# Two decoder layers on one core: the first value projections taken from the un-normalized stream

## The chip, the cores and the metric

One Trainium2 chip, one of its cores. The metric is device microseconds of one execution of the whole kernel. Three runs of the kernel before gave a median of 1659.62 us (1659.4 to 1661.38).

## The reference, cut to what matters

Two layers over 512 tokens of width 1024, each a pre-norm mixer with a plain residual add, and a final norm. Everything is float32.

```python
def rmsnorm(x, g):
    y = x * lax.rsqrt(jnp.mean(x * x, axis=-1, keepdims=True) + EPS)
    return y * g

for i in range(2):
    u = rmsnorm(h, ln_g[i])
    # layer 0, HGRN2:     q, f_pre, i_in (the values), gate = columns of u @ hg_w_in
    #                     chunkwise gated recurrence per head, norm per head, * silu(gate), @ hg_w_out
    # layer 1, attention: for 3 groups (window, dilation): q, k, v = columns of u @ att_w_in
    #                     16 heads of 128; dilated attention, merged over groups, * silu(gate), @ att_w_out
    h = h + y
return rmsnorm(h, final_g)
```

## The kernel before

The stream is held transposed, `hT` with 8 tiles of 128 features by 512 tokens. A float32 product is made of three fp32r matmuls (`split_matmuls`, L428): each operand is split in a high part (ScalarE, a copy that rounds: `split_hi` L741, `u_high` L757) and a low part (VectorE, the difference: `split_lo` L1030, in `norm` L1044). TensorE multiplies high by high, high by low and low by high. The kernel is written engine by engine, each with its instructions in a fixed order, tied by semaphores; no scheduler moves anything.

Weights come in tiles of 128 by 1024 (512 KB), four slots deep, from SyncE's queue: a slot is loaded again when its low part exists (`load_after` L336), and split again when TensorE has used the tile (`wait_tile_done` L285).

The 16 heads go in four groups of four (`quads` L268). Both layers begin with a prologue in which the values of the first four heads are projected: `first_values` (L470) goes over k, the 8 feature tiles, outside and over s, the four results, inside: 3 matmuls for each (k, s), 12 per k, 96 in all. Layer 1 (AT) has three value groups: group 0 by `first_values`, groups 1 and 2 by `values` (L449), which takes s outside and k inside. Groups 1 and 2 take every fourth token. ScalarE copies each result out of PSUM (`copy_values` L750), which counts up `bank_free` of the event's bank. Projections take three banks (`proj`) in turn, by the event's number. A head tile (`head_tile` L436, 24 matmuls) waits for its weight tile and for its bank:

```python
pe.wait_ge(w_ready, number + 1)
pe.wait_ge(bank_free[bank], before)
```

**Opening.** x comes in four tiles of 128 tokens (`load_x` L355), is transposed by TensorE (L554), copied to `hT` by VectorE (L1075), squared and summed by ScalarE (L777); the factor rstd of every token is spread over the partitions by one matmul (L561). Then `norm(0)` makes u = hT * gain * rstd, tile by tile (L1051, L759, L1056), and `first_values` follows it. Midway `bias_rows` (L491) makes the rows of the attention bias; VectorE adds a mask to them (L1109).

**Between the layers.** The last quad's output projection is done in two stages: heads 0 to 2, then head 3 alone, 8 columns of 3 matmuls (`out_projection` L529). VectorE adds each column to `hT` (`add_out` L1217), ScalarE squares it (`square_column` L761), TensorE sums the squares over the features (`sum_squares` L538, one float32 matmul with a matrix of ones). After the eighth sum ScalarE makes rstd (L894, L896), `norm(1)` makes u, and layer 1's `first_values` begins.

## Time and profile before

| | |
|---|---|
| median of three runs | 1659.62 us (1659.4 to 1661.38) |
| the profiled execution | 1660.9 us |
| its span, first to last instruction | 1658.9 us |
| granted TensorE clock, mean | 0.996 |
| TensorE busy | 1634.7 us (99%), 8249 matmuls |
| VectorE busy | 800.4 us (48%) |
| ScalarE busy | 641.3 us (39%) |

A matmul's record is longer than the time it takes from the stream (about 0.39 us against 0.23 from start to start), since records overlap; so times of TensorE are read below from start to start. An instruction with float32 operands has two records. "Granted clock" is the share of full speed, 1.0 for 2.4 GHz and 0.5 for 1.2 GHz.

### The profile page before, as it was taken

What the parts mean: (1) busy time and instruction counts of PE and PEld (TensorE: products, weight loads), DVE (VectorE), ACT (ScalarE), POOL (GpSimd) and SP (SyncE); (2) the same over time, 40 slices, a digit from 0 to 9 for tenths busy, and PEclk for the clock granted to TensorE, in tenths of its full rate; (3) what the DMA queues carried; (4) which work ended last, traced back from release to release, by engine and by line L of the source; (5) the groups of instructions that cost most, each with busy time, mean ns of one, the idle gap of its engine ahead of it and who ended that gap; (6) DMA issues with size and microseconds to landing.
All of it is one profiled execution on the core that took longest, in us unless ns stands there. A gap on an engine that the chain in (4) does not pass through costs nothing.

```text
span 1658.9 us, 22066 instructions
## 1 busy us (share of the span) xinstructions
PE 1634.7 (99%) x8249; PEld 1392.4 (84%) x8249; DVE 800.4 (48%) x1395; ACT 641.3 (39%) x1088; POOL 20.8 (1%) x40
## 2 busy tenths in 40 slices
PE   7999999999999999999999999999999999999997
PEld 5888888888886898888898888899888889888886
DVE  6674675575576424444323444333344432443445
ACT  4553453453454333333332343332343332233333
POOL 0000000000000000000000000000000000000000
PEclk9999999999999999999999999999999999999999
DMA  6523223323221344333333333323323332343311
GB/s 202 177 77 100 78 76 89 89 76 89 82 80 42 89 113 96 79 84 61 104 96 96 96 83 89 78 70 118 91 64 92 96 70 89 114 96 85 82 52 64
DMA packets 247997, 149.46 MB, mean 90 GB/s; under 512 B 47040, under 2 KB 227648, under 8 KB 247920
## 3 DMA queue, kind: packets, MB, share of 16 engines
q1 hardware_dynamic: 203328, 139.69, 30.5%
q0 software_dynamic: 2608, 8.39, 1.5%
q10 hardware_dynamic: 41984, 0.27, 1.3%
q8 instruction: 59, 0.97, 0.2%
q14 instruction: 18, 0.15, 0.0%
HBM read 146.02 MB, written 6.50 MB: 92 GB/s over the span
## 4 chain that ended last, share of the span: by engine, by line
PE 96%; DVE 2%; ACT 1%; issue 0%; DMA 0%; SPq 0%; DVEq 0%; ACTq 0%
PE proj L432 82%; PE inner L699 3%; PE inner L667 2%; PE inner L432 2%; PE inner L687 2%; PE inner L655 1%; PE inner L576 1%; PE inner L599 1%; PE inner L602 1%; PE inner L588 1%; PE inner L581 0%; DMA v<-x 0%; DVE v L1421 0%; PE inner L554 0%; PE inner L541 0%
## 5 line engine op out<-in xcount | busy, mean ns | idle before, releaser
L1036 DVE TENSOR_TENSOR w_lo<-raw,w_hi 128x1024 fp32r<-128x1024 f32 x252 | 308.0, 1223 | 484.0 <-ACT w_hi L748 483.0
L432 PE MATMUL proj<-u_hi,w_hi 128*128 128x512 f32 x1280 | 509.7, 398 | 0.0
L432 PE MATMUL proj<-u_hi,w_lo 128*128 128x512 f32 x1280 | 500.2, 391 | 0.0
L432 PE MATMUL proj<-u_lo,w_hi 128*128 128x512 f32 x1280 | 498.9, 390 | 0.0
L748 ACT ACTIVATE w_hi<-raw 128x1024 fp32r<-128x1024 f32 x252 | 265.3, 1053 | 133.6 <-PE proj L432 118.5
L432 PEld LDWEIGHTS proj<-u_hi,w_lo 128*128 128x128 f32 x1280 | 240.3, 188 | 51.7
L432 PEld LDWEIGHTS proj<-u_lo,w_hi 128*128 128x128 f32 x1280 | 240.9, 188 | 48.0
L432 PEld LDWEIGHTS proj<-u_hi,w_hi 128*128 128x128 f32 x1280 | 240.7, 188 | 47.4
L432 PE MATMUL proj<-w_hi,u_hi 128*128 128x512 f32 x472 | 190.2, 403 | 6.7 <-issue 3.7
L432 PE MATMUL proj<-w_lo,u_hi 128*128 128x512 f32 x472 | 187.5, 397 | 0.0
L432 PE MATMUL proj<-w_hi,u_lo 128*128 128x512 f32 x472 | 187.4, 397 | 0.0
L432 PEld LDWEIGHTS proj<-w_hi,u_hi 128*128 128x128 f32 x472 | 120.8, 256 | 19.7 <-issue 8.9
L432 PEld LDWEIGHTS proj<-w_hi,u_lo 128*128 128x128 f32 x472 | 120.8, 256 | 9.1
L432 PEld LDWEIGHTS proj<-w_lo,u_hi 128*128 128x128 f32 x472 | 121.0, 256 | 8.0
L982 ACT ACTIVATE qk<-proj 128x512 f32<-128x512 f32 x96 | 57.0, 594 | 162.6 <-PE proj L432 162.0
L912 ACT ACTIVATE rows<-rows,negm 128x256 f32<-128x256 f32 (+1 forms) x128 | 61.8, 484 | 140.9 <-DVE negm L1319 130.6
L432 PE MATMUL proj<-y_hi,w_hi 128*128 128x512 f32 x256 | 102.9, 402 | 0.9 <-DVE sg L1125 0.7
L432 PE MATMUL proj<-y_hi,w_lo 128*128 128x512 f32 x256 | 99.8, 390 | 0.0
L432 PE MATMUL proj<-y_lo,w_hi 128*128 128x512 f32 x256 | 99.8, 390 | 0.0
L754 ACT ACTIVATE v<-proj 128x512 f32<-128x512 f32 x59 | 35.1, 596 | 138.8 <-PE proj L432 127.2
L1221 DVE TENSOR_TENSOR hT<-hT,proj 128x512 f32<-128x512 f32 x80 | 54.4, 686 | 65.6 <-PE proj L432 65.4
L432 PEld LDWEIGHTS proj<-y_hi,w_hi 128*128 128x128 f32 x256 | 48.1, 188 | 12.3 <-issue 3.0
(162 smaller groups left out, 1420.9 us busy)
## 6 DMA issues: line engine op xcount, KB each, us to landing
raw<-at_w_in SPq DMA_DIRECT2D x160, 512.0 KB, 4.1
raw<-hg_w_in SPq DMA_DIRECT2D x64, 512.0 KB, 4.2
raw<-hg_w_out SPq DMA_DIRECT2D x16, 512.0 KB, 3.5
raw<-at_w_out SPq DMA_DIRECT2D x16, 512.0 KB, 4.4
v<-x SPq DMA_DIRECT2D x4, 512.0 KB, 6.4
bias_tiles<-ext_rows POOLq DMA_DIRECT2D x1, 2048.0 KB, 11.8
bias_tiles<-ext_rows POOLq DMA_DIRECT2D x2, 1024.0 KB, 17.2
bias_n<-bias_tiles POOLq DMA_DIRECT2D x16, 128.0 KB, 4.0
```

The costliest lines, as they stand in the source:

```text
L432: ins = nc.tensor.matmul(bank[:, :], stationary(a), moving(b), start=(first and n == 0), stop=(last and n == 2))
L576: ins = nc.tensor.matmul(to, aft[:, b * P + c * CH:b * P + (c + 1) * CH], q_steps(b, 0, c, NC - c), start=True, stop=True)
L588: ins = nc.tensor.matmul(p_U[:, b * P:(b + 1) * P], kT[:, b, :], v_sb[0][:, b, h * P:(h + 1) * P], start=True, stop=True)
L667: ins = nc.tensor.matmul(p_S[r // 2][:, ((r % 2) * 2 + i) * P:((r % 2) * 2 + i + 1) * P], qk[:, 2 + 2 * i, s], qk[:, 3 + 2 * i, s], start= ...
L687: ins = nc.tensor.transpose(p_T[n % 2][:, (i % 4) * P:(i % 4 + 1) * P], src, ident[:, :])
L699: ins = nc.tensor.matmul(o, vals, pT[:, i, :], start=(i == 0), stop=(i == len(TILES) - 1), skip_group_check=True)
L748: nc.scalar.activation(w["hi"][:, slot, :], raw[:, slot, :], ACT.Copy).then_inc(hi_ready, 1)
L754: nc.scalar.activation(v_sb[group][:, (e - (0 if q is None else layer.heads)) % ST, :], value_bank(layer, q, e)[:, :], ACT.Copy).then_inc( ...
L912: nc.scalar.activation(probs[:, i, 0:n], probs[:, i, 0:n], ACT.Exp, bias=negm[:, i:i + 1], accum_out=stat[:, i // ST, 1, b:b + 1]).then_in ...
L982: nc.scalar.activation(o, src, ACT.Copy, scale=QSCALE if i in (Q0, Q1, Q2) else 1.0)\
L1036: nc.vector.tensor_tensor(w["lo"][:, slot, :], raw[:, slot, :], w["hi"][:, slot, :].bitcast(F32), ALU.subtract).then_inc(w_ready, 1)
L1221: nc.vector.tensor_tensor(hT[:, k, :], hT[:, k, :], proj[bank][:, :], ALU.add)\
```

## The change

The norm multiplies each token by rstd and each feature by a gain. For a value projection the token is the output's row, so rstd can be applied to the result. The change splits hT * gain, without rstd, for the values of layer 0 and for groups 0 and 1 of layer 1, and gives rstd as a per-partition scale to the copy out of PSUM. The normalized u is made afterwards, for the heads (and group 2), over the same buffers, each pair of tiles when TensorE has used it. In detail:

- x goes in half tiles: 4 transposes, ScalarE copies them to `hT`, VectorE multiplies by the gain, ScalarE and VectorE split. TensorE's transposes and value steps alternate. The gains come by a small load of their own, and the first weight tile is loaded ahead of x's tiles 1 to 3.
- ScalarE's squares of x, rstd and its spreading follow after x's splits. `bias_rows` stands before k = 7.
- Between the layers, squares are added up on VectorE (7 adds). Eight float32 matmuls with one moving column give the sum for every token as a column (`token_sum`), and one of 512 columns the sum spread over the partitions (`feature_sum`).
- Value steps of layer 1 begin between columns 5 and 6 of the output projection's second stage. Group 1 is taken with k outside, too. Group 0 gets banks `inner[0..3]`, the last of group 1 `inner[4]`.

```diff
@@ loads, SyncE @@
             load_x(0)
             sp.dma_start(ident[:, :], consts[:, 0:P]).then_inc(const_loaded[0], 16)
+            sp.dma_start(prow[0:16, P:2 * P], ln_g.rearrange("r (h p) -> (r h) p", p=P)).then_inc(const_loaded[3], 16)
+            load(0, *tile_source(HG, 0, "value", 0, 0))
             for t in range(1, ST):
                 load_x(t)
+            for n in range(1, SLOTS):
+                load(n, *tile_source(HG, 0, "value", 0, n))
...
-            for n in range(SLOTS):
-                load(n, *tile_source(HG, 0, "value", 0, n))
@@ TensorE @@
-            def first_values(layer, u_before):
...
+            def value_step(layer, group, k, s):
+                number, slot, _ = layer.tile(None, 4 * group + k // 2)
+                e = 4 * group + s
+                _, bank, before = layer.event(None, e)
+                if k % 2 == 0 and s == 0:
+                    pe.wait_ge(w_ready, number + 1)
+                if layer is HG and k % 4 == 0:
+                    pe.wait_ge(raw_ready, k + s + 1)
+                elif layer is AT and group == 0 and s == 0:
+                    pe.wait_ge(raw_ready, KT + k + 1)
+                if k == 0 and layer is AT and value_bank(layer, None, e) is proj[bank]:
+                    pe.wait_ge(bank_free[bank], before)
...
+            def token_sum():
+                pe.wait_ge(sq_added, KT - 1)
+                for i in range(2 * ST):
+                    tokens = slice(i * P, (i + 1) * P) if i < ST else slice(i - ST, S, RES)
+                    ins = nc.tensor.matmul(p_ss[:, i:i + 1], sq_sum[:, tokens], ones[:, 0:1], start=True, stop=True)
+            def feature_sum():
+                pe.wait_ge(rcol_step, 1)
+                nc.tensor.matmul(p_ss[:, :], ones[:, :], sq_sum[:, :], start=True, stop=True).then_inc(feature_sums, 1)
...
+                    if last and layer is HG and c == 5:
+                        value_step(AT, 0, 0, 0)
+                        value_step(AT, 0, 0, 1)
...
+            pe.wait_ge(diag_ready, 1)
+            nc.tensor.matmul(p_ss[:, :], ones[:, :], y_f[:, :], start=True, stop=True).then_inc(rstd_spread, 1)
+            bias_rows()
+            for s in range(ST):
+                value_step(HG, 0, 7, s)
@@ ScalarE @@
             def u_high(which, k):
+                wait_tile_done(act, AT if which else HG, None, 4 * which + k // 2, False)
                 act.wait_ge(u_made, which * KT + k + 1)
...
+            def first_value_events(layer, group):
+                last_raw = layer is HG or group == 1
                 for i in range(3):
+                    if last_raw:
+                        u_high(group, 2 * i)
+                        u_high(group, 2 * i + 1)
+                    split_hi(layer, None, 4 * group + i, False)
                 for s in range(ST):
+                    copy_values(layer, None, group, 4 * group + s)
+                if last_raw:
+                    u_high(group, KT - 2)
+                    u_high(group, KT - 1)
+                split_hi(layer, None, 4 * group + 3, False)
...
+            act.wait_ge(feature_sums, 1)
             nc.scalar.activation(rstd[:, :], p_ss[:, :], ACT.Ln, scale=1.0 / D, bias=eps[:, :]).then_inc(rstd_step, 1)
...
+            first_value_events(AT, 0)
+            first_value_events(AT, 1)
+            value_events(AT, None, 2, 0)
@@ VectorE @@
-            norm(0)
...
                 nc.vector.tensor_tensor(ext_sb[:, g * EXT:(g + 1) * EXT], inner[1 + g][0:H, 0:EXT],
                                         relmask_sb[:, g * EXT:(g + 1) * EXT], ALU.add).then_inc(ext_ready, 1)
-            for n in range(3):
-                split_lo(HG, None, n, False)
+            norm(0)
...
+            def last_shares(q):
+                column(0); column(1); raw_low(0); column(2); split_lo(HG, q, HG.heads, True)
+                column(3); column(4); column(5); column(6); raw_low(1); column(7); raw_low(2)
...
+                split_lo(HG, q, HG.heads + 3, True)
+                raw_low(7)
+                add_squares(5)
+                add_squares(6)
+                add_squares(7)
```

(`last_shares` has one call per line in the kernel; its calls are drawn together here.)

Three places of the new order, in which instructions stand otherwise than before.

VectorE, from the end of the parameter arithmetic in the opening. L1109 and L1263 are the mask adds on the rows of `bias_rows`, L1159 and L1164 the two halves of `norm`, L1036 and L1144 `split_lo`. Before:

```order
L1104 TENSOR_SCALAR oml<-lb 128x16 [waits lb_step]
L1109 TENSOR_TENSOR qx<-inner,qx 16x384 [waits ext_done,const_loaded6,lb_step]
L1109 TENSOR_TENSOR qx<-inner,qx 16x384 [waits ext_done] x2
L1036 TENSOR_TENSOR w_lo<-raw,w_hi 128x1024 [waits hi_ready] x3
L1113 MEMSET rows 128x512
```

And with the change:

```order
L1258 TENSOR_SCALAR oml<-lb 128x16 [waits lb_step]
L1263 TENSOR_TENSOR qx<-inner,qx 16x384 [waits ext_done,const_loaded6,lb_step]
L1263 TENSOR_TENSOR qx<-inner,qx 16x384 [waits ext_done] x2
L1159 SCALAR_TENSOR_TENSOR tmp<-hT,param,rstd 128x512 [waits rstd_ready]
L1159 SCALAR_TENSOR_TENSOR tmp<-hT,param,rstd 128x512
L1164 TENSOR_TENSOR u_lo<-tmp,u_hi 128x512 [waits u_hi_ready]
L1159 SCALAR_TENSOR_TENSOR tmp<-hT,param,rstd 128x512 [waits u_ready]
L1164 TENSOR_TENSOR u_lo<-tmp,u_hi 128x512 [waits u_hi_ready]
L1144 TENSOR_TENSOR w_lo<-raw,w_hi 128x1024 [waits hi_ready]
```

The whole of `norm(0)` now stands behind the mask adds, which wait for `bias_rows`; before it stood ahead of the parameter arithmetic.

ScalarE, the copies of the first values in the opening (L754, L817) and what stands ahead of them (L759, L824 are `u_high`; L748, L809 `split_hi`). Before:

```order
L759 ACTIVATE u_hi<-tmp 128x512 [waits u_made] x2
L791 ACTIVATE param<-param 128x48 [waits lb_step]
L811 ACTIVATE ones_r<-ones 128x128 [waits ones_ready]
L748 ACTIVATE w_hi<-raw 128x1024 [waits value_tile_done,loaded0]
L748 ACTIVATE w_hi<-raw 128x1024 [waits value_tile_done,loaded1]
L748 ACTIVATE w_hi<-raw 128x1024 [waits value_tile_done,loaded2]
L754 ACTIVATE v<-proj 128x512 [waits proj_done] x3
```

And with the change:

```order
L889 ACTIVATE rstd<-inner 128x512 [waits rstd_spread]
L916 ACTIVATE ones_r<-ones 128x128 [waits ones_ready]
L824 ACTIVATE u_hi<-tmp 128x512 [waits u_made,value_tile_done] x2
L809 ACTIVATE w_hi<-raw 128x1024 [waits value_tile_done,loaded0]
L824 ACTIVATE u_hi<-tmp 128x512 [waits u_made,value_tile_done] x2
L809 ACTIVATE w_hi<-raw 128x1024 [waits value_tile_done,loaded1]
L824 ACTIVATE u_hi<-tmp 128x512 [waits u_made,value_tile_done] x2
L809 ACTIVATE w_hi<-raw 128x1024 [waits value_tile_done,loaded2]
L817 ACTIVATE v<-proj,cols 128x512 [waits proj_done] x3
```

Six of the eight `u_high` now stand ahead of the copies out of PSUM.

ScalarE, from rstd to layer 1's first value copies. Before:

```order
L894 ACTIVATE rstd<-inner,eps 128x512 [waits ss_done]
L896 ACTIVATE rstd<-rstd 128x512 [waits rstd_step]
L759 ACTIVATE u_hi<-tmp 128x512 [waits u_made] x2
L748 ACTIVATE w_hi<-raw 128x1024 [waits proj_done,loaded2]
L759 ACTIVATE u_hi<-tmp 128x512 [waits u_made] x2
```

And with the change:

```order
L1001 ACTIVATE cols<-inner,eps 128x8 [waits token_sums]
L1004 ACTIVATE cols<-cols 128x8 [waits rcol_step]
L1006 ACTIVATE rstd<-inner,eps 128x512 [waits feature_sums]
L1008 ACTIVATE rstd<-rstd 128x512 [waits rstd_step]
L809 ACTIVATE w_hi<-raw 128x1024 [waits value_tile_done,loaded0,rcol_ready]
L809 ACTIVATE w_hi<-raw 128x1024 [waits value_tile_done,loaded1]
L809 ACTIVATE w_hi<-raw 128x1024 [waits value_tile_done,loaded2]
L817 ACTIVATE v<-inner,cols 128x512 [waits proj_done] x4
```

The splits of group 1's weights and the copies of group 0's values now stand behind a wait for `feature_sum`, which TensorE does just before k = 7.

## Rows read from the trace of the kernel before

**Rows 1.** The page: busy time and share of the span of each engine.
```profile
PE 1634.7 (99%) x8249; PEld 1392.4 (84%) x8249; DVE 800.4 (48%) x1395; ACT 641.3 (39%) x1088; POOL 20.8 (1%) x40
```
**Rows 2.** Waits of TensorE, whole span: us in total, times, longest.
```profile
PE proj L432 <- issue: 3.7, 1, 3.7
PE proj L432 <- DVE u_lo L1056: 3.0, 1, 3.0
```
**Rows 3.** Timeline, 0 to 20 us: start, us, engine, line, operation.
```profile
7.82 5.26 PE L554 MATMUL inner<-ident,v 128*128 128x128 f32 x24 [1.43 <-DMA v<-x]
...
10.45 1.06 ACT L777 ACTIVATE rows<-v 128x1024 f32<-128x1024 f32 x1 [0.19 <-DMA v<-x]
...
15.60 1.41 DVE L1051 SCALAR_TENSOR_TENSOR tmp<-hT,param,rstd 128x512 f32<-128x512 f32 x2
...
17.89 0.77 PE L432 MATMUL proj<-w_hi,u_hi 128*128 128x512 f32 x1 [3.04 <-DVE u_lo L1056]
```
**Rows 4.** Timeline, 22 to 45 us.
```profile
23.12 0.40 PE L432 MATMUL proj<-w_hi,u_hi 128*128 128x512 f32 x1
...
25.29 1.04 ACT L770 ACTIVATE w_hi<-raw 128x1024 fp32r<-128x1024 f32 x1
...
31.41 2.10 PE L496 MATMUL inner<-rows,bias_n 32*16 32x384 f32 x6
...
33.45 0.51 PE L432 MATMUL proj<-w_hi,u_hi 128*128 128x512 f32 x1
...
34.03 2.34 DVE L1036 TENSOR_TENSOR w_lo<-raw,w_hi 128x1024 fp32r<-128x1024 f32 x2
```
**Rows 5.** Timeline of TensorE, first matmuls of head tiles 0 and 1.
```profile
44.50 0.39 PE L432 MATMUL proj<-u_hi,w_hi 128*128 128x512 f32 x1
...
49.94 0.39 PE L432 MATMUL proj<-u_hi,w_hi 128*128 128x512 f32 x1
```
**Rows 6.** Windows: length, busy time and count of each engine, granted clock.
```profile
18.00:20.00 2.00, 2.00 (x5) 1.61 (x6) 2.00 (x3) 1.19 (x2) 0.00 (x0) 0.50 0.63 168
```
**Rows 7.** Timeline between the layers, 526 to 566 us.
```profile
526.76 1.13 PE L541 MATMUL inner<-tmp,ones 128*128 128x512 f32 x2
...
528.42 1.02 PE L541 MATMUL inner<-tmp,ones 128*128 128x512 f32 x2
...
529.51 0.39 PE L432 MATMUL proj<-y_lo,w_hi 128*128 128x512 f32 x1
...
538.31 0.69 ACT L894 ACTIVATE rstd<-inner,eps 128x512 f32<-128x512 f32 x1 [0.27 <-PE inner L541]
539.03 0.63 ACT L896 ACTIVATE rstd<-rstd 128x512 f32<-128x512 f32 x1
...
541.93 0.77 PE L432 MATMUL proj<-w_hi,u_hi 128*128 128x512 f32 x1 [3.66 <-issue]
...
545.64 0.39 PE L432 MATMUL inner<-w_hi,u_hi 128*128 128x512 f32 x1
...
565.37 0.40 PE L432 MATMUL proj<-w_hi,u_hi 128*128 128x512 f32 x1
...
565.57 0.60 ACT L754 ACTIVATE v<-inner 128x512 f32<-128x512 f32 x1
```
**Rows 8.** Groups of instructions, 505 to 542 us: busy, mean ns, idle before.
```profile
L1221 DVE TENSOR_TENSOR hT<-hT,proj 128x512 f32<-128x512 f32 x16 | 10.7, 682 | 4.7 <-PE proj L432 4.6
...
L766 ACT ACTIVATE tmp<-hT 128x512 f32<-128x512 f32 x8 | 5.0, 631 | 11.1 <-DVE hT L1221 7.9 <-PE inner L541 3.1
L1036 DVE TENSOR_TENSOR w_lo<-raw,w_hi 128x1024 fp32r<-128x1024 f32 x4 | 4.9, 1221 | 3.7 <-ACT w_hi L748 3.7
...
L1051 DVE SCALAR_TENSOR_TENSOR tmp<-hT,param,rstd 128x512 f32<-128x512 f32 x3 | 2.2, 751 | 0.4 <-ACT rstd L896 0.4
```
**Rows 9.** Timeline: six records of three small float32 matmuls, and what follows.
```profile
508.48 0.94 PE L588 MATMUL inner<-v,kT 128*128 128x128 f32 x6 [0.52 <-ACT kT L817]
...
509.17 0.48 PE L432 MATMUL proj<-y_hi,w_hi 128*128 128x512 f32 x1
```

More of the change, by code:

```diff
@@ L434, in split_matmuls, with head_tile @@
                 return ins
[L436 removed]
+            def head_tile(layer, q, n, half, first=False):
                 number, slot, _ = layer.tile(q, n)
@@ L533, in out_projection @@
                     out_column(layer, q, tile + c // 2, tile + c + (KT if last else 0), c, (HQ - 1,) if last else range(HQ))
[L534 to L542 removed]
+                    if last and layer is AT and c >= 2:
+                        final_transposes(c - 2)
@@ L556, in _ @@
-            for i in (1, 2, 3):
-                pe.wait_ge(const_loaded[i], 16)
-            nc.tensor.transpose(proj[0][:, 0:80], prow[0:80, 0:P], ident[0:80, 0:80]).then_inc(param_T, 1)
+                if n >= 3:
+                    pe.wait_ge(x_copied, n - 2)
+                for i in range(4):
+                    ins = nc.tensor.transpose(inner[1 + n % 3][:, i * P:(i + 1) * P],
+                                              nat[t][:, half, i * P:(i + 1) * P], ident[:, :])
+                ins.then_inc(x_T, 1)
@@ new lines, in _ @@
+            x_transposes(1, 1)
+            value_step(HG, 0, 0, 3)
+            value_step(HG, 0, 1, 3)
+            x_transposes(1, 2)
+            for s in range(ST):
+                value_step(HG, 0, 2, s)
+                if s == 0:
+                    x_transposes(1, 3)
+            for s in range(ST):
+                value_step(HG, 0, 3, s)
+            for i in (1, 2):
+                pe.wait_ge(const_loaded[i], 16)
+            nc.tensor.transpose(p_ss[:, 0:64], prow[0:64, 0:P], ident[0:64, 0:64]).then_inc(param_T, 1)
@@ L625, in hg_body @@
                     for half in range(2 * HG.per_head):
-                        head_tile(HG, q, HG.per_head * h + half // 2, half % 2)
+                        head_tile(HG, q, HG.per_head * h + half // 2, half % 2, first=(h == 0 and half < 2))
                         if h:
@@ L1290, in hg_body @@
                         split_lo(HG, q, HG.heads + n, last)
-                out_shares(HG, q, last)
+                if last:
+                    last_shares(q)
+                else:
+                    out_shares(HG, q, last)
                 assert links == LINKS_HG, links
             quads(dve, hg_body)
+            for n in range(4):
+                split_lo(AT, None, n, False)
             norm(1)
-            for n in range(AT.pro):
+            for n in range(8, AT.pro):
                 split_lo(AT, None, n, False)
```

287 lines of the change are left out of this document (195 added, 92 removed).

## The prediction

> **What bounds the kernel now.** I read the page first: TensorE is busy for 1634.7 us [rows 1] of a span of 1658.9, and no other engine for half of it. So only what TensorE does not do, or does slowly, can be won. Its waits name two places: 3.0 us in the opening, for the first low part of u, and 3.7 us between the layers [rows 2]. The timeline shows what lies around each. In the opening the first value matmul starts at 17.89 [rows 3], though the last tile of x had landed by 10.4 (ScalarE squares it at 10.45 [rows 3]); between stand rstd, its spreading and the first tile of u. Between the layers the eighth sum of squares, rstd (0.69 + 0.63) and u come one after the other until 541.93 [rows 7]. The windows show the granted clock at 0.50 (1.2 GHz) after the first wait [rows 6], and the starts give the price: 12 matmuls from 17.89 to 23.12 took 5.23 us [rows 3, 4], where 24 take 5.44 in head tile 0, 0.227 each [rows 5], so 2.5 us went there; 9 matmuls from 541.93 to 545.64 took 3.71 instead of 2.04 [rows 7], so 1.7 there. A sum of squares costs TensorE 0.86: from 528.42 to 529.51 less one matmul of 0.23 [rows 7].
>
> **The sum.** I follow TensorE in both places and compare the start of a later instruction: the end of head tile 0 in the opening (49.94 before [rows 5]), and the start of value group 1 between the layers (565.37 before [rows 7]). Behind both the matmuls are the same and no wait of weight is known.
>
> *Opening, up to the bias rows.* The first weight tile now stands ahead of x's tiles 1 to 3, so tile 2 lands when tile 3 did, by 10.4. Three groups of transposes are queued ahead of the first value matmul, which can start at 11.2. Call B the time at which `bias_rows` starts. Until then TensorE does 84 of the 96 matmuls (19.1), 20 transposes (24 took 5.26 [rows 3], at the pace of VectorE's copies, so 0.22 each, 4.4, is the upper end, and half of it the lower; I take 3.0), the parameter transpose (0.2) and rstd's spreading (0.9, as a sum of squares). The clock has fallen by then or falls: 1.7 to 2.5 us as priced, 2.0 taken. Small waits: 0.5. B = 11.2 + 19.1 + 3.0 + 0.2 + 0.9 + 2.0 + 0.5 = 36.9. ScalarE gives nearly the same: from x's arrival on it has 8 copies (0.60), 8 high parts (0.63), 4 squares (1.06, with the read of the sum some 1.25) and 4 weight splits (1.04), so the fourth weight tile's low part is there at about 33.4, and k = 6, the bias and spreading follow. Bounds of B: 34.5 (no low clock, quick transposes) to 39.5 (low clock until the last of x).
>
> *From B to head tile 0.* TensorE does the bias rows (2.04, 31.41 to 33.45 [rows 4]) and k = 7 (2.73) and is free at B + 4.8. But head tile 0 waits for its bank, which is the one of the second value result, and ScalarE copies that only behind six `u_high` and three splits. These follow `norm(0)`, which VectorE starts behind the mask adds. The rows price each link: from the start of the bias rows to VectorE's next work behind the mask adds 2.6 (31.41 to 34.03 [rows 4]); from the first multiply of `norm` to the end of ScalarE's third split behind six high parts 10.7 (15.60 [rows 3] to 25.29 + 1.04 [rows 4]), the same alternation as now; then two copies of 0.60 [rows 7] and 0.06 for the scale read from memory. So head tile 0 starts at B + 14.6, after a wait of 9.8 us. That wait is longer than both waits after which the clock fell, so 2.0 more (1.7 to 2.5) on 5.44. The last two tiles of u are in time, since the head tile needs them 4 us after its start. End of head tile 0: 36.9 + 14.6 + 5.4 + 2.0 = 58.9, against 49.94: **9.0 us lost** (bounds 6.3 to 12.1, by B and the clock).
>
> On the scale, ScalarE's Ln with a bias from memory takes 0.69 and Exp without one 0.63 [rows 7]. The Trainium skill (ScalarE: Activation LUTs, What ACT_TABLE_LOAD costs) gives 93 ns for each such operand. By the row the two copies ahead of head tile 0 take 0.12 longer, by the page 0.19; the measured row is used.
>
> *Between the layers.* Before, from the end of column 2 at 526.52 (the last matmul ahead of 526.76 [rows 7]) to 565.37, 38.85 us held 15 + 96 matmuls, 25.2, and 13.6 of other things: eight sums of squares 6.9, the wait of 3.7, the low clock 1.7, small gaps 1.3. All 13.6 go. What comes:
> - Column 5 waits for VectorE to add column 2, and the first value step for its weight's low part, both behind a split of 1.22 and a `raw_low` of 0.75 [rows 8]: 0.8.
> - `token_sum` waits for the seventh add. VectorE has 8 column adds (0.68), 8 `raw_low` (0.75), 4 splits (1.22) and 7 adds (0.68), 21 us by their records [rows 8], some 19 from start to start as records overlap; and with two buffers for squares an add, a square, a high part and a low part follow each other in a ring between two engines, three times, 1.4 each. From 525.4 that ends at 548.4; TensorE gets there at 547.1: 1.4 (0 to 3).
> - `token_sum` itself: 16 records; 6 such took 0.69 (508.48 to 509.17 [rows 9]): 1.8. `feature_sum`: 0.9.
> - Group 1 waits for ScalarE. Behind `feature_sum` it does Ln and Exp (1.3 [rows 7]), three splits (3.0) and two copies (1.3), and only then is group 1's first bank free, for the count of that bank takes in group 0's second copy: 5.8 with the hops. TensorE has only k = 7 to do, 2.7. Wait: 3.1.
> - Group 2's last weight tile comes 0.2 late, being split behind the last two high parts.
>
> In all 8.2, so **5.4 us gained** (bounds 3.5 to 7.5). The adds and low parts that VectorE gains, and `norm(1)`, lie beside 22 us of group 1; if that cover were gone `norm` would cost its 14 us.
>
> *Sum:* +9.0 - 5.4 = +3.6 us. The profiled execution took 1660.9 (span 1658.9 and 2.0 around it); it would take 1664.5. The median of the runs is 1.3 below it, 1659.6, so I predict **1663.2 us**. A measurement of this kernel can tell a change of 0.2%, 3.3 us, from none.
>
> **The rivals.**
>
> *A second fall of the clock.* The wait ahead of group 1, 3.1 us, is as long as the 3.0 after which 12 matmuls ran at 1.2 GHz [rows 2, 3]. If the clock falls there too it costs 1.7 more: 1664.9; if instead the low clock lasts through x's arrival (B = 39.5, 2.6 later) 1665.8. For it: both waits of this length in the trace ended so. Against: TensorE is dense up to this one. The Trainium skill (TensorE: Matmul & The Clock Gate, Loop structure matters more than you think) says that matmuls between waits run at half clock; the two rows agree with it.
>
> *A quick opening.* B at 34.5 and the short low-clock price give +6.5 there, +1.1 in all: 1660.7. For it: the transposes' 0.22 was the copies' pace, not their own. Against: ScalarE's own sum allows B no earlier than about 36, unless its records overlap more than in the opening before.
>
> *No wait ahead of head tile 0* (the other side). If the copy that frees the bank, and u, do not come behind `norm(0)`'s chain, TensorE goes from k = 7 at B + 4.8 straight on: 9.8 and the clock's 2.0 are not lost, and the change is 8.2 faster, 1651.4. For it: everything else in the change is saving. The point: 3.6 + 3.3 = 6.9 of the 11.8 (wait and clock) have to go, so it decides where the wait, with what the clock costs behind it, is under 4.9 us. Against: the order of instructions on VectorE and ScalarE, which no run can alter, and the 10.7 us of rows 3 and 4.
>
> *The change does less than it says between the layers*: a ring of waits on VectorE holds value steps up too, each k then taking VectorE's 2.8 instead of 2.73 and more; up to 3 us worse, 1666.
>
> **How the numbers follow.** The forecast, +3.6 with its own range 1661.0 to 1665.5, has a chance of 0.45. The second fall or a long low clock 0.20; the quick opening 0.20; no wait ahead of head tile 0 0.08; the slow ring 0.07. The limit of "slower" at 1662.9 cuts the forecast: 0.6 of it lies above. Slower: 0.27 + 0.20 + 0.07 = 0.54, less a little for errors common to all: 0.52. Within 0.2%: 0.18 + 0.20 = 0.38. Faster: 0.08, and 0.02 for what I have not seen: 0.10. The range, 1659.3 to 1668.0, leaves out the fast case and the bounds added one on the other.
>
> **What would show each step.** In the changed profile: the first value matmul at about 11; the bias rows at 36 to 38; TensorE idle for 10 us ahead of head tile 0's first matmul (L442) near 51, released by ScalarE's value copy (L817); VectorE's first `norm` multiply 2.6 us behind the bias rows. Between the layers no idle time ahead of the first value step beyond 1 us, one of about 1.4 ahead of L510 and one of about 3 ahead of group 1, released by ScalarE's L817; the start of group 1 less the end of head tile 0 should be 5.2 smaller than the 515.4 before (the last 0.2 lies behind it). The prediction is wrong if the wait ahead of head tile 0 is under 5 us, or if the time between those two marks shrinks by more than 8 us.

## The result, and the profile after

| | before | after |
|---|---|---|
| time, median of the runs | 1661.01 us (1659.4 to 1661.38, 6 runs) | 1667.79 us (1666.62 to 1669.89, 6 runs) |
| ratio to before, 95% interval | | 1.0044 (1.0034 to 1.0055) |
| profiled execution | 1660.9, span 1658.9 | 1669.1, span 1667.2 |

The change costs 6.8 us by the medians and 8.2 by the two profiled executions; 3.6 was predicted. Ratios are of fast runs only; the one slow run of all is one of `sums_spread`, at 1818.3 us, without which its median is 1663.97. The page after, the busy row: VectorE has 24 operations more [rows 1], TensorE is as busy as before.

```profile
PE 1634.6 (98%) x8252; PEld 1392.3 (84%) x8252; DVE 815.3 (49%) x1419; ACT 653.9 (39%) x1114; POOL 20.9 (1%) x40
```

TensorE's waits after, whole span (us in total, times, longest), answer to [rows 2]. Both waits of before are gone, and one of 9.6 us has come, with two smaller ones.

```profile
PE proj L442 <- ACT v L817: 12.4, 2, 9.6
...
PE inner L510 <- DVE rows L1182: 1.2, 1, 1.2
```

*The opening.* Timelines after, of TensorE, VectorE and ScalarE, against [rows 3 to 5]:

```profile
11.09 0.78 PE L442 MATMUL proj<-w_hi,u_hi 128*128 128x512 f32 x1
...
36.18 2.10 PE L524 MATMUL inner<-rows,bias_n 32*16 32x384 f32 x6
...
38.80 1.39 DVE L1159 SCALAR_TENSOR_TENSOR tmp<-hT,param,rstd 128x512 f32<-128x512 f32 x2
...
49.53 1.83 ACT L817 ACTIVATE v<-proj,cols 128x512 f32<-128x512 f32 x3
...
50.83 0.80 PE L442 MATMUL proj<-u_hi,w_hi 128*128 128x512 f32 x1 [9.59 <-ACT v L817]
...
55.61 0.39 PE L442 MATMUL proj<-u_hi,w_lo 128*128 128x512 f32 x1
```

The first value matmul comes 6.8 us sooner than before, and then the chain runs as it was priced: bias rows at 36.18, the norm 2.62 behind them, ScalarE's value copies at 49.53, head tile 0 at 50.83 after a wait of 9.59. Up to 55 us its matmuls stand 0.43 apart instead of 0.227. The first recurrence starts at 72.27, where before it started at 63.63: **8.6 us lost**. Its row after, and before:

```profile
72.27 1.06 PE L630 MATMUL inner<-qx,aft 128*32 128x128 f32 x32
```

```profile
63.63 1.06 PE L576 MATMUL inner<-qx,aft 128*32 128x128 f32 x32
```

*Between the layers*, against [rows 7]. Timelines after, of TensorE and ScalarE:

```profile
557.27 2.92 PE L510 MATMUL inner<-ones,rows 128*128 128x1 f32 x16 [1.19 <-DVE rows L1182]
560.05 0.47 PE L442 MATMUL inner<-w_hi,u_hi 128*128 128x512 f32 x1
...
561.37 0.63 PE L442 MATMUL inner<-w_lo,u_hi 128*128 128x512 f32 x1
...
564.47 1.02 PE L516 MATMUL inner<-rows,ones 128*128 128x512 f32 x2
...
566.78 2.93 ACT L809 ACTIVATE w_hi<-raw 128x1024 fp32r<-128x1024 f32 x3
...
569.62 2.40 ACT L817 ACTIVATE v<-inner,cols 128x512 f32<-128x512 f32 x4
...
571.01 0.79 PE L442 MATMUL proj<-w_hi,u_hi 128*128 128x512 f32 x1 [2.79 <-ACT v L817]
```

And windows after, of TensorE: the stretch, its length, busy time, matmuls, granted clock, share and rate of the DMA engines.

```profile
557.00:560.00 3.00, 2.73 (x16) 1.00 0.16 59
560.00:561.00 1.00, 1.00 (x5) 0.83 0.00 0
561.00:564.00 3.00, 3.00 (x9) 0.50 0.00 0
...
572.00:574.00 2.00, 2.00 (x6) 0.50 0.90 316
```

The clock falls twice. It is full during the one-column matmuls and at 0.50 (1.2 GHz) soon behind them; then again behind the wait for group 1. Each time the matmuls at 0.43 cost 1.6 to 1.7 us. Layer 1's heads start at 617.90, against 610.48: of the 8.6 us, 7.4 are still there. **Between the layers 1.2 us came back, not 5.4.** The first matmul of the heads after, and before:

```profile
617.90 0.39 PE L442 MATMUL proj<-u_hi,w_hi 128*128 128x512 f32 x1
```

```profile
610.48 0.40 PE L432 MATMUL proj<-u_hi,w_hi 128*128 128x512 f32 x1
```

### The profile page after: what moved, and what is told of

The parts are those of the page before. It is cut to its first block, busy times and chain, and to the rows that moved or that the text cites. A ratio compares the mean times of both kernels' runs of the same rounds, so it can differ in the third digit from the quotient of the medians.

```text
span 1667.2 us, 22147 instructions
## 1 busy us (share of the span) xinstructions
PE 1634.6 (98%) x8252; PEld 1392.3 (84%) x8252; DVE 815.3 (49%) x1419; ACT 653.9 (39%) x1114; POOL 20.9 (1%) x40
## 4 chain that ended last, share of the span: by engine, by line
PE 95%; DVE 3%; ACT 1%; issue 1%; DMA 0%; SPq 0%; DVEq 0%; ACTq 0%
PE proj L442 80%; PE inner L760 3%; PE inner L442 2%; PE inner L728 2%; PE inner L748 2%; PE inner L716 1%; PE inner L630 1%; PE inner L653 1%; PE inner L656 1%; PE inner L642 1%; PE inner L635 0%; DMA v<-x 0%; DVE w_lo L1144 0%; DVE v L1607 0%; DVE rows L1182 0%
## 5 line engine op out<-in xcount | busy, mean ns | idle before, releaser
L1144 DVE TENSOR_TENSOR w_lo<-raw,w_hi 128x1024 fp32r<-128x1024 f32 x252 | 308.0, 1223 | 457.4 <-ACT w_hi L809 456.6
L809 ACT ACTIVATE w_hi<-raw 128x1024 fp32r<-128x1024 f32 x252 | 265.1, 1053 | 120.6 <-PE proj L442 117.1
L442 PE MATMUL proj<-w_hi,u_hi 128*128 128x512 f32 x440 | 178.4, 406 | 3.0 <-ACT v L817 2.8
L442 PE MATMUL proj<-w_lo,u_hi 128*128 128x512 f32 x440 | 175.0, 398 | 0.0
L442 PE MATMUL proj<-w_hi,u_lo 128*128 128x512 f32 x440 | 175.0, 398 | 0.0
L442 PEld LDWEIGHTS proj<-w_hi,u_hi 128*128 128x128 f32 x440 | 114.2, 260 | 14.1 <-DVE w_lo L1144 5.3
L442 PEld LDWEIGHTS proj<-w_hi,u_lo 128*128 128x128 f32 x440 | 114.2, 260 | 8.1
L442 PEld LDWEIGHTS proj<-w_lo,u_hi 128*128 128x128 f32 x440 | 114.5, 260 | 7.0
L817 ACT ACTIVATE v<-proj 128x512 f32<-128x512 f32 x49 | 29.2, 596 | 119.1 <-PE proj L442 107.9
```

The costliest lines, as they stand in the source:

```text
L442: ins = nc.tensor.matmul(bank[:, :], stationary(a), moving(b), start=(first and n == 0), stop=(last and n == 2))
L809: nc.scalar.activation(w["hi"][:, slot, :], raw[:, slot, :], ACT.Copy).then_inc(hi_ready, 1)
L817: nc.scalar.activation(v_sb[group][:, s, :], value_bank(layer, q, e)[:, :], ACT.Copy, scale=cols[:, 8 + ST * group + s:9 + ST * group + s] ...
L1144: nc.vector.tensor_tensor(w["lo"][:, slot, :], raw[:, slot, :], w["hi"][:, slot, :].bitcast(F32), ALU.subtract).then_inc(w_ready, 1)
```

## The experiments

Two kernels first undo one half of the change each; then single parts are moved, and at last two are put together. Each ratio is to the kernel before, in runs on the same chip. A difference to the change in us, where no span is named, compares medians of different chips, on which the kernel before took 1660.68 to 1661.47; such a difference of less than 1 us is not read.

### 1 and 2. One half of the change at a time

`opening_undone` has the whole opening of the kernel before, x's loads, transposes and norm included (a few lines of many):

```
-                raw_u = q is None and group < 2
+                raw_u = layer is AT and q is None and group < 2
...
-            bias_rows()
-            for s in range(ST):
-                value_step(HG, 0, 7, s)
+            pe.wait_ge(param_ready, 1)
+            first_values(HG, 0)
```

> The opening as before, the place between the layers as changed. If the two places simply add up (mine): the changed kernel's profile has head tile 0 end 8.6 us later than before, and the start of layer 1's heads 7.4 us later, so the opening costs 8.6 and the place between the layers gives back 1.3. Then this kernel's head tile 0 ends at 49.9, layer 1's heads begin at about 609.2, and the time is 1.3 us or less under the kernel before, no measurable change. Rival: the two falls of the clock between the layers come from where the opening has shifted that place in time; then without the shift one or both are missing and the kernel is 3 to 4.5 us faster than before.

Measured: 1659.51 us (11 runs; before 1661.47), ratio 0.9990 (0.9981 to 0.9999). The rival is out: both low stretches between the layers are there without the shift, as these windows show, behind the same waits of 1.2 and 2.8 us.

```profile
551.00:554.00 3.00, 3.00 (x10) 0.59 0.00 0
562.00:564.00 2.00, 2.00 (x6) 0.50 1.02 373
```

The heads of layer 1 start at 608.63, 1.9 us sooner than before. Of that, 0.7 was there already at the first recurrence (62.91 against 63.63), ahead of which the two kernels have the same code; 1.1 to 1.2 came between the layers, as in the change.

`between_undone` has the new opening, and between the layers the code of the kernel before:

```
-                raw_u = q is None and group < 2
+                raw_u = layer is HG and q is None and group < 2
...
-                    if last and layer is HG and c == 5:
-
-                        value_step(AT, 0, 0, 0)
-                        value_step(AT, 0, 0, 1)
+                        (sum_squares if layer is HG else final_transposes)(c - 2)
```

> The opening as changed, the place between the layers as before. If the two places add up: 8.6 to 8.7 us slower than the kernel before (about 1669.7), slower than the whole change; head tile 0 starts at 50.8 behind a wait of 9.6. Rival: ScalarE and VectorE run late by the opening's shift only there, and steady work in the loops takes part of it back; then under 6 us.

Measured: 1669.68 us (5 runs), ratio 1.0047 (1.0034 to 1.0061), 7.8 to 8.2 more than before. Its first wait is 9.59 us, as in the change, and the rival of under 6 us is out. So the opening alone loses 8, the part between the layers alone gains 1 to 2, and the two add up to the 6.8 of the change within the noise. Of the two halves the opening went as predicted; the mistake is between the layers.

### 3. Value copies early

The four copies of the first values right behind the first two `u_high` and one split.

```
-                for s in range(ST):
-                    copy_values(layer, None, group, 4 * group + s)
+                    if layer is HG and i == 0:
+                        for s in range(ST):
+                            copy_values(layer, None, group, s)
...
```

> The changed kernel, but ScalarE copies the four first value results behind the first two high parts of u instead of behind six. If the bank is what head tile 0 waits for: it starts near 43.5 instead of 50.8, is then held by u tile by tile (the low parts come every 1.9 us), and ends near 55 instead of 58.6: 3.6 us less, or 2 if the thin stream of matmuls keeps the clock low into head tile 1. Rival: u, not the bank, ends that wait as well; then the start stays near 50 and the time does not change.

Measured: 1667.27 us (1664.89 to 1668.38), ratio 1.0032 (1.0019 to 1.0046), which overlaps with the change's; its span is 1.8 less than the change's. The timelines of this kernel:

```profile
43.31 0.47 PE L442 MATMUL proj<-u_hi,w_hi 128*128 128x512 f32 x1 [2.51 <-DVE w_lo L1148]
...
52.61 0.50 PE L442 MATMUL proj<-u_hi,w_hi 128*128 128x512 f32 x1 [1.44 <-DVE u_lo L1168]
...
61.01 1.06 ACT L809 ACTIVATE w_hi<-raw 128x1024 fp32r<-128x1024 f32 x1 [3.35 <-DMA raw<-hg_w_in]
...
68.98 1.06 PE L630 MATMUL inner<-qx,aft 128*32 128x128 f32 x32 [0.91 <-DVE qx L1346]
```

Head tile 0 starts 7.5 us sooner and ends 4.3 sooner (54.27 against 58.58): it now waits for the norm inside itself, column by column. Then ScalarE waits 3.35 us for a weight tile that it had waited 0.85 for in the change, and the first recurrence is 3.3 sooner. Of that 1.5 are lost between the layers, 0.85 of it behind the one-column matmuls: there the clock fell at once, and the stretch from them to `feature_sum` took 5.27 us (556.93 to 562.20) instead of 4.42. So the first theory had the start and the end of head tile 0 (43.5 and 55 expected), and the norm as the next limit. It did not have the weights behind it, nor that the clock's price between the layers can change with nothing moved there.

### 4. Weight splits ahead of the sums

Between the layers, ScalarE's three splits for group 1 ahead of its wait for `feature_sum`.

```
+            for i in range(3):
+                split_hi(AT, None, i, False)
             act.wait_ge(feature_sums, 1)
...
-                    split_hi(layer, None, 4 * group + i, False)
+                    if last_raw:
+                        split_hi(layer, None, 4 * group + i, False)
```

> The changed kernel, but between the layers ScalarE splits group 1's first three weight tiles ahead of the wait for feature_sum instead of behind it. If the wait ahead of group 1 is ScalarE's queue: its copies of group 0 are then done by about the end of k = 7, the wait of 2.8 us shrinks under 0.5, and the fall of the clock behind it (1.6 us) goes with it: 4 us less. Rival: the clock falls there for another reason (the falls follow the load, not the wait); then only 2.5 us less.

Measured: 1664.29 us (10 runs), ratio 1.0016 (1.0007 to 1.0025), 3.5 less than the change and 4.6 by the span. Group 1 starts without a wait, and the windows show the clock full there, but still low behind `token_sum`:

```profile
567.67 0.60 PE L442 MATMUL proj<-w_hi,u_hi 128*128 128x512 f32 x1
```

```profile
561.00:564.00 3.00, 3.00 (x10) 0.58 0.22 20
...
568.00:570.00 2.00, 2.00 (x10) 1.00 0.35 132
```

The second fall belonged to the wait; with the wait it is gone, as the first theory says.

### 5. Two of the eight token sums

This kernel leaves out the sums of six of the eight columns, so it sizes a cost and is no version to use.

```
-                for i in range(2 * ST):
+                for i in (0, ST):
```

> The changed kernel, but token_sum issues only two of its eight matmuls with one moving column (the first of the plain and the first of the strided four), so the row factors of six of the eight value row blocks are not computed: that part is left out. It sizes two things that the sum had wrong or did not hold. Theory (each record costs 0.175 us, and the clock falls behind token_sum because of the long stretch of one-column matmuls): 4 records instead of 16 cost 0.7 us instead of 2.8, the wait of 1.2 us for the squares stays, and the clock stays at 1.00 behind them, so 2.1 + 1.6 = 3.7 us less than the change (1667.8), about 1664.1; the second fall, at group 1, stays. Rival (the clock falls because of the wait of 1.2 us ahead of them, whatever their number): low clock behind token_sum as before, so only 2.1 less, about 1665.7. A third reading, that the cost is one fixed price for the switch of kind and not one for each record, would leave more than 2 us between the start of token_sum and the next value step.

Measured: 1664.91 us (10 runs), ratio 1.0025 (1.0016 to 1.0035). Its timeline, and one window:

```profile
557.94 0.85 PE L510 MATMUL inner<-ones,rows 128*128 128x1 f32 x4 [1.19 <-DVE rows L1182]
558.64 0.47 PE L442 MATMUL inner<-w_hi,u_hi 128*128 128x512 f32 x1
```

```profile
560.00:564.00 4.00, 4.00 (x18) 1.00 0.00 0
```

Four records take 0.70 us, 0.175 each, so the price is one for each record. The wait of 1.2 is the same as in the change and the clock stays full behind it: the wait alone does not lower it, so what does is the long row of one-column matmuls, alone or together with the wait; the next run tells which. The spans differ by 3.6, the medians by 2.9; the theory said 3.7.

### 6. Sums later

On `splits_first`, both sums moved back.

```
-                if k == KT - 2:
-                    token_sum()
                 if k == KT - 1:
-                    feature_sum()
+                    token_sum()
...
+                    if k == KT - 1 and s == 1:
+                        feature_sum()
```

> splits_first (1664.3) with both sums moved back: token_sum behind step 6 of group 0 instead of ahead of it, feature_sum in the middle of step 7. Nothing is left out. The last add of squares ended 1.2 us after TensorE came for it, and step 6 takes 2.8 us, so both theories expect that wait at 0. Theory (the stretch of one-column matmuls is what lowers the clock): the 16 records still take 2.8 us with the granted clock at about 0.5 to 0.6 behind them, and the time is 1.2 less than splits_first, about 1663.1. Rival (the wait of 1.2 us ahead of them made the clock fall): no low stretch between 555 and 568 us, and 2.8 less, about 1661.5. What speaks against both would be a new wait of group 1 for the value copies, as feature_sum and with it the rstd row come 2.5 us later: ScalarE's copies then start late and TensorE waits for the first of them.

Measured: 1664.40 us (8 runs), ratio 1.0024 (1.0013 to 1.0035), no gain over `splits_first`. Timeline and window:

```profile
558.95 2.81 PE L510 MATMUL inner<-ones,rows 128*128 128x1 f32 x16
561.62 0.78 PE L442 MATMUL inner<-w_hi,u_hi 128*128 128x512 f32 x1
...
568.22 0.60 PE L442 MATMUL proj<-w_hi,u_hi 128*128 128x512 f32 x1 [1.31 <-ACT v L817]
```

```profile
562.00:565.00 3.00, 3.00 (x9) 0.55 0.00 0
```

No wait stands ahead of the one-column matmuls now, and the first matmul behind them already takes 0.78: the clock fell without any wait. That they are float32 is not enough for it either: in the change the six float32 records of `bias_rows`, with 384 columns each (36.18 to 38.22), are followed by matmuls 0.23 apart. The gain of 1.2 is taken back by the new wait of 1.31 for the value copies, which the expectation had named as what would speak against both theories' times. The Trainium skill (TensorE: Matmul & The Clock Gate, Loop structure matters more than you think) holds that matmuls that stand back to back stay at full clock. For the 512-column ones the traces here agree (the twelve ahead of `token_sum` in the change are 0.227 apart); this row of one-column matmuls, back to back on both sides, is a counterexample.

### 7. Sums spread

On `splits_first`, two one-column matmuls behind each row block of step 6.

```
...
                 for s in range(ST):
                     if k or s >= 2:
                         value_step(AT, 0, k, s)
+                    if k == KT - 2:
+                        token_sums_of(s)
```

> splits_first (1664.3) with token_sum cut in four: two of its one-column matmuls behind each of the four row blocks of step 6, feature_sum where it was. Nothing is left out. Theory (clock falls because one-column matmuls stand in a row): the low stretch between 555 and 568 us is gone, 1.6 us; most of the wait of 1.2 us too, since one row block (0.7 us) now stands ahead of the first of them; and the records cost what they cost, so about 2.3 less than splits_first, near 1662.0. If the 0.175 us of a record is a weight load with nothing beside it, part of it hides behind the 512-column matmuls here (at most one of the four records of each group, 4 x 0.175 = 0.7), down to 1661.3. Rival (what costs is the weight load of a one-column matmul wherever it stands, and the clock falls with it too): no more than 0.7 less than splits_first.

Measured: 1664.01 us (10 runs), ratio 1.0020 (1.0010 to 1.0030). Timeline and windows:

```profile
557.02 0.85 PE L510 MATMUL inner<-ones,rows 128*128 128x1 f32 x4 [0.51 <-DVE rows L1186]
557.72 0.47 PE L442 MATMUL inner<-w_hi,u_hi 128*128 128x512 f32 x1
...
562.37 1.13 PE L517 MATMUL inner<-rows,ones 128*128 128x512 f32 x2 [0.36 <-ACT cols L1003]
...
567.93 0.59 PE L442 MATMUL proj<-w_hi,u_hi 128*128 128x512 f32 x1 [1.69 <-ACT v L818]
```

```profile
556.00:560.00 4.00, 3.49 (x19) 1.00 0.30 111
560.00:564.00 4.00, 3.64 (x17) 1.00 0.00 0
```

The mechanism is confirmed and the forecast of the time, 1662.0 or less, is a miss. The low clock is gone and the first wait down to 0.51. But the three splits still stood behind the token sums on ScalarE, so the value copies came late, and TensorE waited 0.36 and 1.69 us. A record costs 0.175 here too, behind the wait (557.02 to 557.72) and between wide matmuls: from 557.72 to 559.10 stand three 512-column matmuls, 0.68, and four records, 0.70. The wide matmuls beside it hide nothing of it.

### 8. Norm early

In the opening: rstd's spreading behind step 5, two columns of `norm` and a split ahead of the mask adds, the value copies behind column 3.

```
             for k in (4, 5, 6):
                 for s in range(ST):
                     value_step(HG, 0, k, s)
-            pe.wait_ge(param_ready, 1)
-            pe.wait_ge(diag_ready, 1)
-            nc.tensor.matmul(p_ss[:, :], ones[:, :], y_f[:, :], start=True, stop=True).then_inc(rstd_spread, 1)
+                if k == 5:
+                    pe.wait_ge(param_ready, 1)
+                    pe.wait_ge(diag_ready, 1)
+                    nc.tensor.matmul(p_ss[:, :], ones[:, :], y_f[:, :], start=True, stop=True).then_inc(rstd_spread, 1)
...
```

> The changed kernel with the opening's norm moved ahead: the matmul that spreads rstd stands behind step 5 instead of step 6, VectorE makes its first two normed columns and splits head tile 0's weights ahead of the three adds of the bias rows, and ScalarE copies the values behind column 3 and split 1 instead of behind all of them. Nothing is left out. Theory (head tile 0 was late because three things stand in a row ahead of it, bias rows, then the norm, then the value copies): rstd is copied at about 34 instead of 36.3, the norm starts at 34.6 instead of 38.8, head tile 0 starts at about 41 to 42 without a long wait, at full clock, and ends near 50, as in the kernel before (49.94); the whole is 6.5 to 8.5 less than the change, 1659.3 to 1661.3. Rival (the copies and the norm only covered a wait for the weights of the later head tiles, as copies_early hints, which started head tile 0 7.5 us sooner and had 3.1 us left of it at the first recurrence, with ScalarE waiting for a weight tile's transfer at 61.0): head tile 0 is as early as above but the first recurrence (L630) stands 3 to 4 us ahead of the change's 72.3, not 8, and the time is 2.5 to 4 less.

Measured: 1661.94 us (10 runs), ratio 1.0008 (0.9998 to 1.0017), 5.9 less than the change. Its timelines:

```profile
34.56 1.42 DVE L1167 SCALAR_TENSOR_TENSOR tmp<-hT,param,rstd 128x512 f32<-128x512 f32 x2 [1.66 <-ACT rstd L890]
...
43.26 0.50 PE L442 MATMUL proj<-u_hi,w_hi 128*128 128x512 f32 x1 [1.71 <-ACT v L818]
...
62.53 1.06 ACT L810 ACTIVATE w_hi<-raw 128x1024 fp32r<-128x1024 f32 x1 [3.05 <-DMA raw<-hg_w_in]
...
65.86 1.06 PE L631 MATMUL inner<-qx,aft 128*32 128x128 f32 x32
```

The first recurrence is 6.4 us sooner than in the change. The wait for weights is there (3.05 us on ScalarE), but no wait of TensorE follows from it. So the theory holds in the main and the rival, that the weights would set the pace, does not; the theory's size is a little high, 6.5 to 8.5 against 5.9, as head tile 0 still waits 1.71 us for its bank and starts at 43.26 instead of 41 to 42. At the first recurrence 2.2 us to the kernel before remain: head tile 0's last columns wait for the norm, and it ends at 52.16 instead of 49.94.

### 9. One release less

```
-                    pe.wait_ge(bank_free[bank], before)
+                    pe.wait_ge(bank_free[bank], before - 1)
+                elif k == 0 and layer is AT and e == 2 * ST - 1:
+                    pe.wait_ge(rstd_step, 1)
```

> The changed kernel with group 1's value matmuls waiting for one release less of their PSUM bank. The banks of group 0 are others here, but their copies are counted on the same semaphores, so group 1 waits for a copy whose bank it does not write; its last row block, which does write the bank of the sums, waits instead for ScalarE's read of them. Nothing is left out. In the changed kernel group 1 started at 571.0, 2.8 us after TensorE came for it, behind the first value copy, while the low half of its first weight tile was ready at 569.0. Theory (the wait is the counted copy, and the second low-clock stretch hangs on its length): the wait falls from 2.8 to 0.8 us, the clock stays up behind it, 2.0 + 1.7 = 3.7 us less than the change (1667.8), about 1664.1, as splits_first. Rival (the wait of 0.8 still lowers the clock): 2.0 less, 1665.8. Rival (what it waits for is the weight split all along): no more than 0.3 less.

Measured: 1664.42 us (10 runs), ratio 1.0022 (1.0013 to 1.0031), 3.4 less than the change. Timeline:

```profile
568.90 0.63 PE L442 MATMUL proj<-w_hi,u_hi 128*128 128x512 f32 x1 [0.91 <-DVE w_lo L1146]
```

```profile
570.00:572.00 2.00, 2.00 (x11) 1.00 0.91 249
```

The wait is 0.91 with another releaser, and the clock is at 1.00 in the window behind it. The 2.8 us were a wait for a copy whose bank group 1 does not write; 1.9 of them go with it, and for the other 0.9 the weight's low part is not there yet either. `splits_first` takes all of the 2.8 by another way, with the count as it was: there the copies are in time.

### 10 and 11. All mended

Both have, between the layers: the three splits ahead of ScalarE's wait for the token sums, the one-column matmuls in pairs behind blocks 1 to 3 of step 6 and block 0 of step 7, `feature_sum` behind block 1 of step 7, and the wait of run 9.

```
+                    if (k, s) in ((6, 1), (6, 2), (6, 3), (7, 0)):
+                        token_sums_of((s - 1) % ST)
+                    if (k, s) == (7, 1):
+                        feature_sum()
...
+            for i in range(3):
+                split_hi(AT, None, i, False)
             act.wait_ge(token_sums, 1)
```

> The opening of the kernel before with the changed part between the layers, that part mended in four places: three weight splits of ScalarE ahead of its wait for the token sums; the one-column matmuls two at a time behind row blocks 1 to 3 of step 6 and block 0 of step 7, so that no wait for the squares stands ahead of them; feature_sum behind block 1 of step 7; and group 1 not waiting for the counted copy. Nothing is left out. From opening_undone (1659.5), if what the single runs showed adds up: 1.2 for the wait, 1.6 for each of the two low-clock stretches, 2.8 for the wait of group 1, together 7.2, and the one-column records stay at 2.8: 1652.3, which would be 8 us under the kernel before. Rival (a wait or a low stretch moved later, as in sums_later and sums_spread, where group 1 waited 1.3 and 1.7 us): 3 to 5 less than opening_undone, 1654.5 to 1656.5.

Measured: **1652.07 us** (1651.43 to 1653.28, 5 runs; before 1660.91), ratio 0.9948 (0.9934 to 0.9962), 0.5% faster than the kernel before. Its windows between the layers:

```profile
545.00:550.00 5.00, 5.00 (x25) 1.00 0.34 107
550.00:555.00 5.00, 5.00 (x25) 1.00 0.65 205
555.00:560.00 5.00, 5.00 (x21) 1.00 0.30 113
```

TensorE is busy in all of it, at full clock. The first expectation, 1652.3, was met: what the single runs showed adds up, once no wait takes the place of the one removed. From the first recurrence (64.18) to the heads (603.14) it takes 6.8 us less than `opening_undone`, where 7.2 were expected.

> norm_early (1661.9), with two value copies one column earlier, and the same mended part between the layers. Nothing is left out. In norm_early the waits and low stretches between the layers are those of the change, so if they go as in best_old_opening: 7.2 less, and up to 0.9 from ScalarE's copies no longer standing ahead of split 1 (VectorE waited 0.87 us for it), 1653.8 to 1654.7. The two openings then compare on equal terms: theory, the new opening remains about 2 us behind the old one, since norm_early's first recurrence stood 2.2 us behind that of the kernel before. Rival: with split 1 earlier the chain of norm, split and transfer closes that gap, and the two are within 0.7 us of each other.

Measured: 1654.70 us (1652.59 to 1655.73, 5 runs), ratio 0.9961 (0.9947 to 0.9974). It is at the upper end of the 1653.8 to 1654.7 expected; the new opening stays 2.6 us behind the old one, as the theory had it (about 2), and the rival that the gap closes is out. Starting head tile 0 at 40.84, 2.4 us sooner than in `norm_early`, bought nothing: it waited 1.44, 0.42 and 1.41 us for the low parts of u, and behind the last of these the clock was low, which in `norm_early` it was not. The last low part came 1.5 us sooner (49.01 against 50.52), the low clock cost 2.3, and the first recurrence is 0.8 later (66.66 against 65.86). The row, and windows of this kernel and of `norm_early`:

```profile
49.01 0.80 PE L442 MATMUL proj<-u_hi,w_hi 128*128 128x512 f32 x1 [1.41 <-DVE u_lo L1178]
```

```profile
48.00:52.00 4.00, 2.99 (x7) 0.50 0.98 313
```

```profile
48.00:52.00 4.00, 2.45 (x9) 1.00 0.98 321
```

## Why the prediction was right about the sign and wrong about the size

*The opening: right.* First value matmul 11.2 predicted, 11.09 measured; B, the start of the bias rows, 36.9 and 36.18; from the bias rows to the norm 2.6 and 2.62; head tile 0 B + 14.6 and B + 14.65; its wait 9.8 and 9.6; the clock behind it 2.0 and about 2.3. B came 0.7 sooner mostly because the low clock ahead of it cost 1.4 (six matmuls at 0.43 and no more) where 2.0 stood. In all 9.0 us predicted and 8.6 measured. `between_undone` shows the loss alone. `norm_early` shows that its cause is what was named, the order ahead of the copies, by winning 6.4 of the 8.6 back. The rival without that wait can be dropped.

*Between the layers: the failed step.* Predicted was a list of 8.2 us that comes; its prices for `token_sum` and for the clock, which it put at nothing, are what failed. Measured:

- Column 5 and the first value step: 0.3 each, 0.6 in all, where 0.8 stood.
- The wait ahead of `token_sum`: 1.2, where 1.4 stood.
- **`token_sum` itself: 2.8, where 1.8 stood.** I priced a record at 0.115 us by six records that had 128 moving columns [rows 9], as if one column could only cost less. It costs 0.175, shown by 4 records in 0.70 and 16 in 2.8 (2.7 in `sums_later`). The nearest row by type and kind was not nearest in shape, and it should have been one end of a range. The Trainium skill (TensorE: Matmul & The Clock Gate, LDWEIGHTS (loading the stationary operand)) gives the number of columns over 1.2 as the nanoseconds of a weight load, which makes 107 for 128 columns; an estimate of 1.7 us for 16 records by that page is too low too, and the measured 2.8 decides.
- **The clock behind `token_sum`: 1.6, where nothing stood, and no rival named it.** I looked for falls behind waits only. `two_columns` (same wait, no fall) and `sums_later` (no wait, the same fall) show that the row of 16 one-column records causes it. At which number between 4 and 16 it sets in, no run shows.
- The wait ahead of group 1: 2.8, where 3.1 stood. Its cause was named rightly, the count of the bank with group 0's second copy: group 1 starts at 571.01, when the second of the four copies that begin at 569.62, each about 0.6, is done. Run 9 shows it for 1.9 of the 2.8.
- **The clock behind that wait: 1.7.** This was the rival with a chance of 0.20. The trace had two waits of such a length and low clock behind both, so the rows were for it and only "TensorE is dense up to this one" against; it should have been in the forecast. The last weight tile of group 2, put at 0.2, I did not measure apart.

With `feature_sum` at 0.9 this makes 11.6 of the 13.6 that go, so 2.0 gained by this list, and 1.2 by the starts of the heads; the other 0.8 is what the rows of the waits leave out. From start to start, the first matmul behind a wait or behind float32 matmuls comes later than the wait's own row says: the trace gives 0.9 instead of 0.6 for column 5 and the first value step, 1.35 instead of 1.2 ahead of `token_sum`, 1.7 instead of 1.6 for the clock behind it, and 2.95 instead of 2.8 ahead of group 1, together 0.7 of it. The three bold terms are 1.0, 1.6 and 1.7 too low, 4.3 in all; the other terms were 0.9 too high, and the 0.8 was not in the list: together the miss of 4.2 in this half. By the prediction's own mark, from the end of head tile 0 to the start of group 1, the time shrank by 3.0 (571.01 less 58.58, against 515.4), not by 5.2; the clock's 1.7 lies behind that mark.

*What stays open.* The profiled spans differ by 8.3, the starts of layer 1's heads by 7.4. From there to the last matmul record the kernels, whose code is the same there, took 1038.7 and 1039.6, so differences below 1 us over that stretch have no cause that these runs can show. The same holds ahead of it: `opening_undone`, the kernel before and `best_old_opening` have the same opening and the same wait of 3.04 us in it, and start head tile 0 at 43.78, 44.50 and 45.05, as the clock stays low behind that wait for more or fewer matmuls.

## What to carry to other kernels

Price a wait that you remove with what stands right behind it: head tile 0 started 7.5 us sooner and ended only 4.3 sooner, because the norm was next in the row, and a gain between the layers was taken back by a new wait twice (`sums_later`, `sums_spread`) until the splits and the release were mended with it. A reduction by one-column matmuls cost 0.175 us a record here, and a row of 16 cost 1.6 more by the clock behind it; four records at a time between wide matmuls left the clock full. And when results move to other PSUM banks, look at what the release counts still count: a wait may hold for a bank that is no longer written, as 1.9 us did here.

## What the runs showed of the hardware that was not expected

- A float32 matmul record with one moving column took 0.17 to 0.175 us from start to start, in a row of 16 (2.8 and 2.7), of 4 (0.70), and between 512-column matmuls (0.70 for 4); the six records with 128 columns took 0.115 each [rows 9].
- The granted clock fell to 0.50 behind 16 of them in a row, with a wait ahead (change) and without (`sums_later`, where the window of 0.55 holds the recovery too); behind 4 it stayed at 1.00, four times over when spread.
- Waits of 0.9, 1.3, 1.7 and 1.7 us ahead of 512-column matmuls left the clock at 1.00; those of 2.5 (`copies_early`), 2.8, 3.0 and 3.7 (before) and 9.6 were followed by 0.50. But waits of 1.4, 0.4 and 1.4 close together in one head tile were followed by 0.50 in one kernel (`best_new_opening`), and those of 0.5, 0.4 and 1.4 at the same place in `norm_early` were not.
- The same fall began 0.9 us behind the last one-column record in one kernel (cost 1.6) and at once in another (0.85 more), and behind the same wait of 3.04 us in the old opening the low clock lasted for 8, 12 and 14 matmuls in three kernels: its price varies with nothing changed around it.
